# Moving filler matmuls, low halves and one output DMA between engines in a three-layer transformer kernel

## What is computed

```python
# first block
xn = rms_norm(h, mix_norm)
q, k, v, cb, cc, cx, ga, gc = split(xn @ w_in + b_in)
attn = sliding_window_attention(q, k, v, sinks)      # 8 heads, 2 key/value groups, window 128
conv = cb * causal_depthwise_conv(cc * cx, conv_w)   # 3 taps
merged = sigmoid(ga) * (attn @ w_attn_branch) + sigmoid(gc) * (conv @ w_conv_branch)
h = h + merged @ w_out
up = causal_depthwise_conv(rms_norm(h, ffn_norm) @ w_up, ffn_conv_w)
gate, val = split(up)
h = rms_norm(h + (silu(gate) * val) @ w_down, final_norm)
# then two hybrid layers: chunked attention with a relative bias, and retention
for l in range(2):
    aq, ak, av, ag, rq, rk, rv, rg = split(rms_norm(x) @ w_in_2[l])
    y = concat(chunked_rel_attention(aq, ak, av) * silu(ag),
               chunkwise_retention(rotary(rq), rotary(rk), rv) * silu(rg))
    x = x + y @ w_out_2[l]
out = rms_norm(x, final_gain)
```

## Time and profile before

| | us |
|---|---|
| median of 3 runs | 1185.54 (1185.33 to 1186.76) |
| the profiled execution's own time | 1185.57 |
| its span (first to last record) | 1183.8 |
| PE busy | 1172.0 |
| DVE busy | 896.3 |
| ACT busy | 577.1 |
| POOL busy | 246.5 |

### The profile page before, as it was taken

One profiled execution on the slowest core, in us unless ns is written; L12 is line 12 of the kernel. 1 busy time (PEld: TensorE's weight loads), 2 busy tenths in 40 slices (PEclk: granted clock), 3 DMA queues, 4 the chain that ended last, 5 costly groups with the idle time before them and its releaser, 6 DMA issues.

```text
span 1183.8 us, 14982 instructions
## 1 busy us (share of the span) xinstructions
PE 1172.0 (99%) x5539; PEld 983.4 (83%) x5539; DVE 896.3 (76%) x1482; ACT 577.1 (49%) x972; POOL 246.5 (21%) x223
## 2 busy tenths in 40 slices
PE   9999999999999999999999999999999999999997
PEld 7887788888888888888888888899888888898886
DVE  6889855656776487546776788997897878998876
ACT  6677623324343243325444477764335577753432
POOL 0220399931100000000003602101502311112200
PEclk9999999999999999999999999999999999999999
DMA  6455533333331533233332347663223376663521
GB/s 197 128 170 170 158 90 102 94 98 98 125 94 54 155 90 101 78 111 103 89 107 76 120 134 224 195 175 92 72 72 107 107 205 178 190 185 116 143 89 72
DMA packets 216717, 146.81 MB, mean 124 GB/s; under 512 B 6250, under 2 KB 205380, under 8 KB 216516
## 3 DMA queue, kind: packets, MB, share of 16 engines
q1 hardware_dynamic: 216628, 145.86, 42.3%
q10 hardware_dynamic: 16, 0.00, 0.0%
HBM read 127.49 MB, written 18.35 MB: 123 GB/s over the span
## 4 chain that ended last, share of the span: by engine, by line
PE 87%; DVE 7%; ACT 3%; issue 2%; DMA 1%; POOL 0%; DVEq 0%; SPq 0%; ACTq 0%
PE ps L191 86%; ACT a_p L161 1%; DVE tmp L164 1%; DVE wlo L164 1%; DVE a_p L178 1%; DVE a_pd L182 1%; DVE x1h L167 1%; DVE a_zc L167 0%; ACT whi L161 0%; DMA raw<-in_w_in_dram 0%; DMA xtm<-in_x_dram 0%; DVE smx L164 0%; ACT x1h L161 0%; PE ps L194 0%; DVE a_pt L164 0%
## 5 line engine op out<-in xcount | busy, mean ns | idle before, releaser
L161 ACT ACTIVATE whi<-raw 128x1024 fp32r<-128x1024 f32 (+2 forms) x199 | 206.9, 1045 | 293.5 <-PE ps L191 282.4
L164 DVE TENSOR_TENSOR wlo<-raw,whi 128x1024 fp32r<-128x1024 f32 (+2 forms) x193 | 252.1, 1311 | 43.7 <-ACT whi L161 43.2
L191 PE MATMUL ps<-x0h,whi 128*128 128x512 f32 x1008 | 254.8, 391 | 1.2 <-ACT whi L161 1.2
L191 PE MATMUL ps<-x0h,wlo 128*128 128x512 f32 x1008 | 254.4, 391 | 0.0
L191 PE MATMUL ps<-x0l,whi 128*128 128x512 f32 x1008 | 254.1, 390 | 0.0
L191 PEld LDWEIGHTS ps<-x0h,whi 128*128 128x128 f32 x1008 | 187.4, 188 | 39.6 <-ACT whi L161 1.5
L191 PEld LDWEIGHTS ps<-x0l,whi 128*128 128x128 f32 x1008 | 188.0, 188 | 38.8 <-DVE x0l L167 0.2
L191 PEld LDWEIGHTS ps<-x0h,wlo 128*128 128x128 f32 x1008 | 187.9, 188 | 38.4
L164 POOL TENSOR_TENSOR sums<-sums,sq 128x512 f32<-128x512 f32 x28 | 43.0, 1549 | 446.2 <-ACT sq L161 446.2
L191 PE MATMUL ps<-x1h,wlo 128*128 128x512 f32 x304 | 82.1, 389 | 0.0
L191 PE MATMUL ps<-x1l,whi 128*128 128x512 f32 x304 | 82.1, 389 | 0.0
(11 more groups left out here) (213 smaller groups left out, 1636.4 us busy)
## 6 DMA issues: line engine op xcount, KB each, us to landing
raw<-in_w_in_dram SPq DMA_DIRECT2D x98, 512.0 KB, 4.1
raw<-in_w_up_dram SPq DMA_DIRECT2D x44, 512.0 KB, 3.8
raw<-in_w_out_dram SPq DMA_DIRECT2D x24, 512.0 KB, 3.6
turned<-b_pd SPq DMA_DIRECT2D x16, 640.0 KB, 3.5
raw<-in_w_down_dram SPq DMA_DIRECT2D x16, 512.0 KB, 3.7
b_px<-turned SPq DMA_DIRECT2D x32, 160.0 KB, 3.4
b_p<-turned SPq DMA_DIRECT2D x32, 160.0 KB, 3.6
turned_a<-a_pd SPq DMA_DIRECT2D x6, 512.0 KB, 2.6
```

Of the source, the lines that this page charges most:

```text
L161: return AC.put(lambda e: e.activation(o, i, func, **kw), after, AC, 1)
L164: return on.put(lambda e: e.tensor_tensor(o, a, b, op), after, on, 1)
L191: return PE.put(lambda e: e.matmul(o, l, r, start=start, stop=stop), after, PE if mark else None, 1)
```

## The change

Five edits:

1. The ones are multiplied 9 times instead of 8, and 2 more such products stand before the first weight product.
2. The high half of feature tile 1 is made by DVE instead of ACT, and DVE makes it before the low half of tile 0.
3. The values' transposes go through PSUM bank 5 instead of 3.
4. The low halves of the attention units' `a_pt` go from DVE to POOL, and the low halves of the six convolution tiles from POOL to DVE.
5. The DMA of the first half of the last output tile is issued by ACT instead of SP.

```diff
         for j in range(4):
-            for n, m in enumerate((14 + j, 10 + j, 6 + j)):
-                plan_fm(win, m, on_pool=j < 3 and n != 1)
+            for m in (14 + j, 10 + j, 6 + j):
+                plan_fm(win, m)
...
-        for _ in range(8):
-            mm(PS[7][:, 0:128], ONES[:, :], ONES[:, :], True, True, after=t_ones)
+        def busy(n):
+            for _ in range(n):
+                mm(PS[7][:, 0:128], ONES[:, :], ONES[:, :], True, True, after=t_ones)
+
+        busy(9)
...
-            X0.th[k] = act(hi, PS[bank][:, :], scale=MIX(k), after=[tp, t_mix])
-            X0.tl[k] = stt(lo, PS[bank][:, :], MIX(k), f32(hi), ALU.mult, ALU.subtract, after=[tp, X0.th[k]])
+            if k == 1:
+                X0.th[k] = ts(hi, PS[bank][:, :], MIX(k), None, ALU.mult, after=[tp, t_mix])
+            else:
+                X0.th[k] = act(hi, PS[bank][:, :], scale=MIX(k), after=[tp, t_mix])
+
+            def low():
+                X0.tl[k] = stt(lo, PS[bank][:, :], MIX(k), f32(hi), ALU.mult, ALU.subtract, after=[tp, X0.th[k]])
+
+            if k:
+                if k == 1:
+                    lows.pop()()
+                low()
+            else:
+                lows.append(low)
...
                 w_hi, w_lo = W.split_in_two(256)
+                busy(2)
                 w0 = W.take()
...
-            free = claim(3)
+            free = claim(5)
...
-            tl = tt(lo, px, f32(hi), ALU.subtract, after=[t_px, th, tfree])
+            tl = tt(lo, px, f32(hi), ALU.subtract, after=[t_px, th, tfree], on=PO)
...
-                t_done = dma(out[0][128 * t:128 * t + 128, 0:512], ob[:, t, 0:512], d_out, after=tf)
+                t_done = dma(out[0][128 * t:128 * t + 128, 0:512], ob[:, t, 0:512], d_out, after=tf, on=AC)
```

More of the change, by code:

```diff
@@ L574, in x_features @@
             return tp, rest
-        rests = {}
+        rests, lows = {}, []
         for c in range(4):
@@ L710, in evac_v @@
             yield 4
-            free = claim(3)
+            free = claim(5)
             for b in range(4):
-                tp = tr(PS[3][:, 128 * b:128 * b + 128], t[:, 128 * b:128 * b + 128], IDENT,
+                tp = tr(PS[5][:, 128 * b:128 * b + 128], t[:, 128 * b:128 * b + 128], IDENT,
                         after=[a, free], mark=b == 3)
@@ L716, in evac_v @@
             yield 1
-            src = PS[3][:, :].rearrange("p (b g d) -> p g b d", b=4, g=2)
+            src = PS[5][:, :].rearrange("p (b g d) -> p g b d", b=4, g=2)
             for g in range(2):
@@ L723, in evac_v @@
             vv_tok.extend([th, tl])
-            bank_free[3] = [th, tl]
+            bank_free[5] = [th, tl]
         def evac_q(j):
```

## The result

The changed kernel takes **1281.3 us** (median of 4 runs, 1280.78 to 1282.11) against 1185.78 us for the kernel before, timed beside it: **1.0797 times, with an interval of 1.0784 to 1.0811**. It is 95.5 us slower. Predicted were 1284.2 us (1278 to 1299), slower with a chance of 0.97. The execution that the trace shows took 1282.11 us itself, so that traces differ by 96.5 us where medians differ by 95.5.

The account below looks back on a forecast made before the run. PE was taken as the bound, with any wait behind 123 us added whole; 96.9 + 1.9 + 0 + 0.2 + 0 - 0.4 = 98.6 on 1185.57 gave 1284.2 us, range 1278 to 1299.

Parts of the forecast that it names:

- The eighth low half: Eighth attention unit: PE waits for a low half behind 73 rotary-table instructions on POOL, until 236.4 instead of 139.55, +96.9 us.
- the nine rounds: Rounds in POOL's rotary-table chain: 9.10 us each with DVE idle, 81.9 us in all, against 95.0 before.
- DVE in 32 to 130 us: DVE before the positions' load: six weight tiles' low halves exchanged for seven units' halves, net 0, ends -2 and +7.5.
- The pace: POOL's rotary-table chain during PE's wait: runs at its quiet pace, 9.10 us a round, because DVE is idle.
- Rival 1: POOL's rotary-table chain keeps its old pace, +111.5 us for the wait, 1298.8 us in all; chance 0.08.
- The clock: Behind PE's long wait: PE resumes at 1.2 GHz for 3.8 us, losing 1.9 us, ends 0 and 3.8.
- The first seven low halves: Units before the eighth, low halves on POOL: -3.3 to +6 us, swallowed by the later wait, so 0.
- Opening: Kernel start, edits 1 and 2: more products of ones, one high half on DVE; +0.2 us, ends -0.6 and +1.0.
- bank: Values' transposes through PSUM bank 5 instead of 3: 0, as PE doesn't wait at the scores.
- last DMA: Kernel end, edit 5: with the first DMA on ACT's queue the second starts at once, -0.4 us; end 0.
- Rival 2: DVE falls behind before 127 us, positions land late, POOL's chain starts up to 7.5 us later: 1291.7 us; chance 0.07.
- rival 3: Eighth half doesn't wait for the chain and the seven others remove PE's 3.3 us: 1182.1 us; chance 0.02.

Follow-up runs that it names:

- the fillers: Changed kernel with 405 or 392 overwritten matmuls of 512 columns on PE ahead of the eighth unit's own: 1281.45 us with 405, 1279.74 us with 392.
- the mended kernels: Changed kernel with the eighth low half back on DVE (1187.25 us), or with the rotary tables recorded two gate projections later (1187.3 us).
- the same kernel without the fillers: Changed kernel with the low halves of units 6, 7 and 8 on DVE, without nine spare-bank matmuls at unit 6: 1185.45 us, 0.9987 of the kernel before.
- 405 fillers: Changed kernel with 405 matmuls of 512 columns, result overwritten, on PE ahead of the eighth unit's own four: 1281.45 us.

## Why the prediction was right

- **The eighth low half, +96.9 us.** Right in kind: the place behind 73 instructions, shown by three runs (another engine, another order, a shorter chain). Measured 233.93 - 139.55 = 94.4, against 96.9. Of the 2.5 us too much, 1.6 are the positions, which landed at 134.35 and not at 135.95, and 0.9 are the nine rounds (81.04 against 81.9), because TENSOR_TENSOR took 1.26 us, not 1.29. Prologue (11.3) and end (4.9) were as taken. With the clock's 2.1 this makes up the 96.5 us between the two spans.
- **DVE in 32 to 130 us, 0.** Mis-sized by those 1.6 us. Unit 5's half is ready at 110.48 (108.07 + 2.41) in the changed kernel, at 112.42 before; PE comes to unit 6 1.4 us earlier (120.11 against 121.50), and the positions' load is issued 1.4 us earlier (128.87 against 130.26). The term allowed for -2. One reading under it was off: the slowed pair of DVE operations of the earlier trace rows (44.58 to 49.61) had two of POOL's low halves beside it, the one of 46.67 and one of 43.75 to 46.13. The exchange was near even all the same. That pair takes 1.53 us in the changed kernel, 3.5 less, and beside POOL's low halves of units 5 and 7 two stretches came, of some 1.5 and 2.0 us by the 0.75 of one such operation:
```profile
108.80 2.23 DVE L167 SCALAR_TENSOR_TENSOR tmp<-tmp,cols,a_zc 128x512 f32<-128x512 f32 x1
126.83 3.55 DVE L167 SCALAR_TENSOR_TENSOR a_zc<-a_zc,cols 128x512 f32<-128x512 f32 x2
```
  What moved the load is that PE's 1.50 us wait at unit 5 went.
- **The pace.** Rival 1, the old pace, fell: 9.00 us a round with DVE idle, 111.6 us for the chain where DVE works. The Trainium skill's rule of shared SBUF interfaces ("GPSIMD Engine Reference", Key points) agrees with this: the changed kernel's trace has POOL's TENSOR_TENSOR at 1.26 us beside an idle DVE, the kernel before's has it at up to 2.16, as in 203.43 to 205.59, which begins within a DVE low half (202.10 to 204.43).
- **The clock, +1.9.** From PE's return to its last product 1274.39 - 233.93 = 1040.46 us (to DVE's read of the last result), before 1177.89 - 139.55 = 1038.34: +2.1, and the fillers show the cause. That the size was met owes something to luck. The term took the opening's burst (3.78 us) as the time at half speed, but the granted clock over that burst reads 1.00:
```profile
1.00:5.00 4.00, 3.96 (x17) 3.64 (x17) 0.01 (x1) 1.49 (x2) 0.00 (x0) 1.00 0.68 209
```
  No run tells what slows the burst, and the time at 0.50 behind three long waits was 3.4, 4.4 and 5.6 us, half of which is lost. The sign that PE's busy time grows by no more than the clock's 2 us failed: it grew by 4.0. The 2.1 us are in it, 1.4 behind unit 6 and 1.0 of products of ones (0.43 + 0.61).
- **The first seven low halves, 0 (swallowed).** Right for the changed kernel, where they cost nothing beside the long wait. What I missed: that PE's two waits at unit 6 lower the clock (granted 0.57 in 122 to 126 in the changed kernel). That is swallowed there too, but it is what keeps the mended kernels over the kernel before.
- **Opening +0.2, bank 0, last DMA -0.4.** The first is neither shown nor refuted by the times, and by the prediction's own argument it belonged in the sum only as far as it moves the positions' load, since the rest is swallowed before 139.5. The bank was never tried by itself. The last was wrong: 0. Its end ("if the transfer and not the issue is what is waited for") is what happened.
- **Rival 2** (DVE behind) and **rival 3** (faster) didn't occur. Rival 3's condition was right: with the half ahead of the chain, the time is back.

## What to carry to other kernels

An engine's list is run from top to bottom, and a list that the code records in program order is not in order of need: before work is moved to an idle engine, look at what is recorded between its neighbours there, for every instance and not for the first. Here the moves of units 1 to 5 and 7 left PE without a wait of its own for them, the sixth made a wait of 1.0 us into one of 2.1 with a lower clock behind it, and the eighth stood behind 97 us of work that nobody needed soon. And a wait of PE that looks too short to matter can cost as much again by the clock behind it; nine matmuls into a spare bank inside that wait cost nothing here, while 405 in the long wait ran some 3 us past its end.

## What was not expected

- **A wait of 3.3 us in two pieces costs 1.4 to 2.8 us more by the clock.** In the kernel before 0.8 and 1.0 us at the same place leave the clock at 1.00 in the profiled execution, while other executions of kernels with the same waits have it fall there: with edit 5 alone PE waits 0.80 and 1.02, and the granted clock is 0.92 over 123 to 145; with edits 1 and 2 alone it is 0.79, 1.02 and the same clock. With PE kept busy there, 11 times lie within 1.1 us, where the same kernel without the fillers spreads over 2.4.
```profile
123.00:145.00 22.00, 21.92 (x89) 17.90 (x90) 20.02 (x35) 14.37 (x24) 8.50 (x5) 0.92 0.52 156
```
- **POOL is a little faster while PE stands.** TENSOR_TENSOR of 128x512 takes 1.26 us and the 128x1024 low half 2.34 in the wait; with 405 fillers on PE the same two take mostly 1.28 to 1.29 and 2.40, with DVE idle in both. No run tells why.
